# A two-layer decoder trunk in one kernel: the order of the last matmuls of each stage, and the variance of one half of the tokens by ScalarE

## The chip, the cores and the metric

The kernel runs on one core of a Trainium2 chip. The metric is the device time of one launch in microseconds (us), the median of several runs. TensorE (PE in the profile) does the matmuls, VectorE (DVE) and ScalarE (ACT) work elementwise, GpSimd (POOL) does small elementwise work and some loads, SyncE (SP) issues the weight loads. Each engine takes its own instructions in order; they wait for each other on semaphores.

## The reference, cut to what matters

The input is 256 tokens by 1024 channels in float32. Two layers run, each a sandwich of three steps; after each step there is a residual sum and a LayerNorm:

```python
for i in range(2):
    x = post_norm(x, 0.5 * swiglu(x, gate[i, 0], up[i, 0], down[i, 0]), g[i, 0], b[i, 0])
    mix = pool_mixer(...) if i == 0 else swa_sink_attention(...)
    x = post_norm(x, mix, g[i, 1], b[i, 1])
    x = post_norm(x, 0.5 * swiglu(x, gate[i, 1], up[i, 1], down[i, 1]), g[i, 2], b[i, 2])
# post_norm(x, sub) = layer_norm(alpha * x + sub), alpha = sqrt(2)
# swiglu(x) = (silu(x @ gate) * (x @ up)) @ down, 1024 -> 2816 -> 1024
```

So there are four SwiGLU stages (f = 0 to 3), one pooling mixer, one attention mixer, and six norms (n = 0 to 5): n = 0 after f = 0, n = 1 after the pooling, n = 2 after f = 1, n = 3 after f = 2, n = 4 after the attention, n = 5 at the very end.

## The kernel before, in words

**Tokens and banks.** The 256 tokens are two halves, t = 0 and t = 1, of 128 tokens, one to each partition. The sum of a stage stands in four PSUM banks, `ACC[t][h]`, h being the half of the 1024 output columns. `xn[:, t, :]` is the residual stream.

**Units.** The 2816 hidden channels are 22 units of 128. For each unit PE multiplies gate and up weights (`gate_up`), ACT and DVE make silu times up, then a high and a low part of it (`h_hi_of`, `h_lo_of`), and PE multiplies by the down weights (`ffn_down`, which calls `down`: three matmuls for each t and h, high by high, high by low, low by high). Weights are split likewise: ACT writes the high part of one half unit (`g_split`, L551) and DVE the low part (L860); for down weights L559 and L864. Unit 21 and units 0 and 1 are direct ones: ACT takes its silu from PSUM (L568), DVE multiplies (L875), ACT makes the high part (L578), DVE the low part (L880).

**The order is written by hand** for each engine, and so is each place of a `g_split`. In stages f = 1 and 2, unit 1 of the next stage's weights has its first half split last in unit 21: ACT's turn comes behind `h_hi_of`, DVE's behind `h_lo_of`. ACT splits the second half too, and POOL makes that half's low part (L384). ACT's `g_split` of that unit waits, before its first half, for

```python
after(act, g_used, G0[f] + (-1, 0, 0, 2)[u] if u < 4 else G - 1 + 4 * it)
```

where f and u are the next stage and 1; `g_used` reaches `G0[f]` with the last matmul of `gate_up` of unit 21 of the stage that ends. For the attention's weights the number is `G_QKV + 0`, with the same meaning.

**The end of a stage on PE** (last_u = 18), in order: the down matmuls of unit 19, t = 0, h = 1; of unit 18 for t = 1; of units 20 and 21 for t = 0, first h = 0 and then h = 1; of units 19 to 21 for t = 1, first h = 0 and then h = 1. The first down matmul of unit 21 waits for `h_lo_of(21)`. Then come the transposes of the normed t = 0 (L1328) and the next stage's first product over t = 0, `gate_up_tokens` (L1261), then the transposes of t = 1. After f = 0, PE runs the pooling: `means` (L1043) and `maps` (L1057) for t = 0 and 1. ACT copies the results of `means` into SBUF (L674). In the attention the last products are `wo(k)`, which also call `down`.

**A norm on DVE**, for t = 0 and then for t = 1: residual sum of h = 0 (L942), `bn_stats` of it (L948), the same for h = 1, `bn_aggr` (L952), variance plus epsilon (L953), which releases POOL's power of -1/2 (L450), the centring of both halves (L960, in place), the scaling of both halves (L973), which releases PE's transposes. `link` makes DVE wait for the instruction just issued. For t = 1 of all norms but the first and last, `x_lo` of t = 0 (L989) lies between variance and centring. ACT copies the transposed halves for the next stage (L630).

Of the kernel before, what the change touches and what calls it, by code (L numbers as in the profile page):

```python
# [21 lines left out]
P = 128  # L22
D = 1024
# [3 lines left out]
TT = S // P  # L27
UNITS = F // P
# [41 lines left out]
def trunk_kernel(nc, x, positions, ln_g, ln_b, w_gate, w_up, w_down, pool_w, pool_b, pool_scale,  # L70
# [8 lines left out]
    with ExitStack() as ctx:  # L79
# [28 lines left out]
        cst = sb("cst", [P, 4, P])  # L108
        stats = sb("stats", [P, 2, 6])
        mv = sb("mv", [P, 2, 2])  # L110
        rstd = sb("rstd", [P, 2, 2])
# [11 lines left out]
        xf = qT[:, :, :].rearrange("p k s -> p (k s)").rearrange("p (t k s) -> p t k s", t=TT, k=KT)  # L123
        uT = [v.rearrange("p (k s) -> p k s", k=KT) for v in (q_sb[:, :, :].rearrange("p t c -> p (t c)"), kT[:, :, :].rearrange("p g s -> p (g s)"))]
        pool_s = q_sb[:, :, :].rearrange("p t c -> p (t c)")
        pool_bs = kT[:, :, :].rearrange("p g s -> p (g s)")
# [27 lines left out]
        h_lo_done = sem("h_lo_done")  # L154
        acc_done = sem("acc_done")
        stat_done = sem("stat_done")
        cen_done = sem("cen_done")
# [379 lines left out]
        def _(act):  # L537
# [70 lines left out]
            def first_units(f):  # L608
# [9 lines left out]
                d_split(D0[f] + 2)  # L618

            def channel_major(e, between=None):  # L620

                for t in range(TT):
# [28 lines left out]
            for f in range(FFNS):  # L651
# [16 lines left out]
                if f == 0:  # L668

                    act.wait_ge(d_scaled, POOL_UNITS)  # L670
                    for t in range(TT):
# [7 lines left out]
                if f == 2:  # L679
                    channel_major(QKV_EVENT)  # L680
                    attention_act(act, g_split, d_split)
                    enter(3)

        def rotary_tables(dve, link):
# [158 lines left out]
        def _(dve):  # L843
# [38 lines left out]
            def unit(f, u, it=0):  # L882
# [53 lines left out]
            def residual_sum(n, t, h):  # L936
# [3 lines left out]
                if n == 4:  # L940
                    dve.wait_ge(res_done, t + 1)
                link(dve.scalar_tensor_tensor(xn[:, t, HALVES[h]], ACC[t][h], coef, xn[:, t, HALVES[h]], ALU.mult, ALU.add))  # L942

            def variance(n, t):

                for h in range(2):
                    residual_sum(n, t, h)
                    last = dve.bn_stats(stats[:, h, :], xn[:, t, HALVES[h]])  # L948
                    if h == 0:
                        note(last)  # L950
                link(last)
                link(dve.bn_aggr(mv[:, t, :], stats[:, :, :].rearrange("p a b -> p (a b)")))  # L952
                dve.tensor_scalar(rstd[:, t, 0:1], mv[:, t, 1:2], EPS / ALPHA ** 2, None, ALU.add).then_inc(stat_done, 1)  # L953

            def centre(n, t):

                if t == 0:
                    dve.wait_ge(scale_in, 16 * (n + 1))
                for h in range(2):
                    dve.scalar_tensor_tensor(xn[:, t, HALVES[h]], xn[:, t, HALVES[h]], mv[:, t, 0:1], ln_scale(n)[:, HALVES[h]],  # L960
                                             ALU.subtract, ALU.mult).then_inc(cen_done, 1)

            def scale(n, t):
# [7 lines left out]
                for h in range(2):  # L971
                    dve.wait_ge(cen_done, 4 * n + 2 * t + h + 1)
                    dve.scalar_tensor_tensor(xn[:, t, HALVES[h]], xn[:, t, HALVES[h]], rstd[:, t, 1:2], ln_offset(n)[:, HALVES[h]],  # L973
                                             ALU.mult, ALU.add).then_inc(xn_done if n < 5 else y_done, 1)
# [59 lines left out]

        def pool_pe(pe):

            def means(t, src, columns, first, last):

                for k in range(KT):
                    if k % 4 == 0 and t == src:  # L1040
# [3 lines left out]
                                    start=first and k % 4 == 0, stop=last and k % 4 == 3)  # L1044
                    if t == 0 and k == 0:
# [4 lines left out]
            def maps(t):  # L1050
                if t == 0:
                    pe.wait_ge(d_scaled, POOL_UNITS)
                for g in range(len(WINDOWS)):
                    if g % 2 == 0:
                        pe.wait_ge(u_sb, 2 * t + g // 2 + 1)
                    for j in range(2):
                        ins = pe.matmul(ACC[t][g // 2][:, (g % 2) * GC:(g % 2 + 1) * GC], uT[t][:, 2 * g + j, :],  # L1057
                                        pool_raw(j)[:, g * GC:(g + 1) * GC], start=j == 0, stop=j == 1)
                    if g % 2 == 1:
                        ins.then_inc(acc_done, 1)  # L1060
# [9 lines left out]
        def attention_pe(pe, three, down, transposes):  # L1070

# [94 lines left out]

            transposes(e, 0)
            qkv(0, 0, 0, part=0, d_counted=True)
            qkv(0, 1, 0, part=0)
# [46 lines left out]
            for h in range(2):  # L1216
                for k in range(5, 8):
                    wo(k, (1,), hs=(h,))
# [3 lines left out]
        def _(pe):  # L1222
# [28 lines left out]
            def gate_up_tokens(f, t):  # L1251
# [6 lines left out]
                for k in range(KT):  # L1258
                    if k % 4 == 0:
                        pe.wait_ge(x_hi_done, 4 * e + 2 * t + k // 4 + 1)  # L1260
                    pe.matmul(out_, xT_hi[:, k, tok], w_hi[:, :, :, k, :], start=k == 0, stop=False)  # L1261
                    pe.matmul(out_, xT_hi[:, k, tok], w_lo[:, :, :, k, :], start=False, stop=False)  # L1262
# [51 lines left out]
            def ffn_down(f, u, ts=(0, 1), it=0, hs=(0, 1)):  # L1314
# [6 lines left out]
                down(E, hT_hi[:, E % D_SLOTS, :], hT_lo[:, E % D_SLOTS, :], ts, u == 0, final, it, hs)  # L1321

            def transposes(e, t, used=0):

# [9 lines left out]
            for f in range(FFNS):  # L1334
                e = FFN_EVENT[f]

                transposes(e, 0, used=(0, 2, 1, 1)[f])
                if f == 0:
# [28 lines left out]
                ffn_down(f, last_u + 1, (0,), hs=(1,))  # L1367
                ffn_down(f, last_u, (1,))
                for h in range(2):
                    for u in (last_u + 2, last_u + 3):  # L1370
                        ffn_down(f, u, (0,), hs=(h,))
                for h in range(2):
                    for u in range(last_u + 1, UNITS):
                        ffn_down(f, u, (1,), hs=(h,))
                if f == 0:
                    pool_pe(pe)
                if f == 2:
                    attention_pe(pe, three, down, transposes)

# [38 lines left out]
```

## Time and profile before

| what | value |
|---|---|
| median of 3 runs | 860.23 us (860.13 to 860.37) |
| the profiled execution | 860.7 us |
| its span in the trace | 858.9 us |
| granted TensorE clock, mean | 0.997 |
| PE busy | 841.1 us, 98% of the span |
| PE weight loads busy (beside the matmuls) | 711.5 us, 83% |
| DVE busy | 562.8 us, 66% |
| ACT busy | 419.3 us, 49% |
| POOL busy | 45.8 us, 5% |
| chain that ended last | PE 91%, DVE 4%, ACT 1%, DMA 1% |

The span runs from the first to the last instruction on record; the profiled execution's own time is 1.8 us longer and lies 0.5 us above the median. Busy shares are means over the whole span. The ends of matmuls are modelled: two that overlap by the record stand about 0.23 us apart from start to start for 512 columns, and that is what one costs.

### The profile page before, as it was taken

The page shows a single profiled execution, that of the slowest core. Times are in us where ns is not written, and L with a number is a line of the kernel's source. Part 1 is how long each engine was busy: PE and PEld are TensorE (multiplying, and loading weights), DVE is VectorE, ACT ScalarE, POOL GpSimd, SP SyncE. Part 2 cuts the span into 40 slices and gives each one's busy share as a digit, 9 for nine tenths or more (in the row PEclk, how much of TensorE's full clock was granted, in tenths as well). Part 3 has the DMA queues.
Part 4 walks back from the last instruction along what each step waited for, and adds up shares of the span by engine and source line. Part 5 has one row for each costly group of instructions (what it writes and reads, how often), then busy time and mean ns, then how long its engine had stood idle before and what let it go on. Part 6 is the DMA issues. An engine that isn't in the chain of part 4 may idle for free.

```text
span 858.9 us, 12145 instructions
## 1 busy us (share of the span) xinstructions
PE 841.1 (98%) x4484; PEld 711.5 (83%) x4484; DVE 562.8 (66%) x777; ACT 419.3 (49%) x651; POOL 45.8 (5%) x59
## 2 busy tenths in 40 slices
PE   7999999999999999999999999999999999999995
PEld 6888888888888888887888888887766888888885
DVE  2785655669846565668665565669898855655656
ACT  2554454552535455454445454554665544454540
POOL 0060000013000000002000000011001000000000
PEclk9999999999999999999999999999999999999998
DMA  9997555392755655556656556553454565465501
GB/s 277 348 325 243 177 195 178 116 294 101 250 192 180 203 188 195 172 179 228 205 158 229 168 177 206 185 196 123 167 167 154 172 224 196 154 229 168 182 1 49
DMA packets 116142, 162.17 MB, mean 189 GB/s; under 512 B 3936, under 2 KB 97632, under 8 KB 116112
## 3 DMA queue, kind: packets, MB, share of 16 engines
q1 hardware_dynamic: 112656, 152.06, 53.1%
q0 software_dynamic: 2496, 9.44, 3.3%
q8 instruction: 19, 0.31, 0.1%
q10 hardware_dynamic: 960, 0.27, 0.1%
q14 instruction: 11, 0.09, 0.0%
HBM read 160.70 MB, written 1.05 MB: 188 GB/s over the span
## 4 chain that ended last, share of the span: by engine, by line
PE 91%; DVE 4%; SPq 1%; DMA 1%; ACT 1%; issue 1%; POOL 0%; DVEq 0%; ACTq 0%
PE ps L1295 29%; PE ps L1293 17%; PE ps L1226 10%; PE ps L1227 10%; PE ps L1228 10%; PE ps L1292 4%; PE ps L1261 1%; DMA raw_g<-in_ffn_w_up 1%; PE ps L1262 1%; PE ps L1266 1%; PE ps L1092 1%; PE ps L1095 1%; PE ps L1101 1%; SPq L322 1%; PE ps L1328 1%; PE ps L1057 1%
## 5 line engine op out<-in xcount | busy, mean ns | idle before, releaser
L1295 PE MATMUL ps<-xT,g_hi 128*128 128x512 f32 x1064 | 379.3, 396 | 0.0
L1293 PE MATMUL ps<-xT,g_lo 128*128 128x256 f32 x1216 | 314.2, 279 | 0.0
L1293 PEld LDWEIGHTS ps<-xT,g_lo 128*128 128x128 f32 x1216 | 229.2, 188 | 12.5
L860 DVE TENSOR_TENSOR g_lo<-raw_g,g_hi 128x1024 fp32r<-128x1024 f32 x179 | 220.4, 1235 | 24.9 <-ACT g_hi L551 24.9
L1295 PEld LDWEIGHTS ps<-xT,g_hi 128*128 128x128 f32 x1064 | 199.7, 188 | 41.2
L870 DVE TENSOR_TENSOR gu<-ps,gu 128x512 f32<-128x512 f32 x76 | 52.5, 691 | 221.9 <-ACT gu L574 221.9
L551 ACT ACTIVATE g_hi<-raw_g 128x1024 fp32r<-128x1024 f32 x184 | 192.1, 1052 | 5.2 <-DMA raw_g<-in_ffn_w_up 3.6
L574 ACT ACTIVATE gu<-ps 128x512 f32<-128x512 f32 x76 | 45.6, 600 | 273.5 <-PE ps L1295 273.5
L1226 PE MATMUL ps<-d_hi,hT_hi 128*128 128x512 f32 x352 | 137.5, 391 | 0.0
L1227 PE MATMUL ps<-d_lo,hT_hi 128*128 128x512 f32 x352 | 137.0, 389 | 0.0
L1228 PE MATMUL ps<-d_hi,hT_lo 128*128 128x512 f32 x352 | 137.0, 389 | 0.0
L864 DVE TENSOR_TENSOR d_lo<-raw_d,d_hi 128x1024 fp32r<-128x1024 f32 x96 | 117.3, 1224 | 5.9 <-ACT d_hi L559 5.8
L559 ACT ACTIVATE d_hi<-raw_d 128x1024 fp32r<-128x1024 f32 x96 | 99.8, 1046 | 4.7 <-DMA raw_d<-in_ffn_w_down 4.7
L1228 PEld LDWEIGHTS ps<-d_hi,hT_lo 128*128 128x128 f32 x352 | 66.1, 188 | 14.2
L1227 PEld LDWEIGHTS ps<-d_lo,hT_hi 128*128 128x128 f32 x352 | 66.1, 188 | 14.0
L1226 PEld LDWEIGHTS ps<-d_hi,hT_hi 128*128 128x128 f32 x352 | 66.1, 188 | 10.6
L1292 PE MATMUL ps<-xT,g_hi 128*128 128x512 f32 x152 | 60.4, 397 | 1.0 <-DVE g_lo L860 1.0
L578 ACT ACTIVATE hT_hi<-hf_sink 128x256 fp32r<-128x256 f32 x82 | 34.3, 418 | 34.5 <-DVE hf_sink L875 34.2
L880 DVE TENSOR_TENSOR hT_lo<-hf_sink,hT_hi 128x256 fp32r<-128x256 f32 x82 | 34.4, 420 | 3.4 <-ACT hT_hi L578 3.4
L875 DVE TENSOR_TENSOR hf_sink<-gu 128x256 f32<-128x256 f32 x76 | 33.3, 438 | 1.0 <-ACT gu L568 1.0
L568 ACT ACTIVATE gu<-gu 128x256 f32<-128x256 f32 x76 | 30.9, 407 | 3.2 <-DVE gu L870 3.2
L1292 PEld LDWEIGHTS ps<-xT,g_hi 128*128 128x128 f32 x152 | 28.5, 188 | 4.3 <-DVE g_lo L860 1.5
(155 smaller groups left out, 662.0 us busy)
## 6 DMA issues: line engine op xcount, KB each, us to landing
raw_d<-in_ffn_w_down SPq DMA_DIRECT2D x87, 512.0 KB, 4.0
raw_g<-in_ffn_w_gate SPq DMA_DIRECT2D x43, 1024.0 KB, 5.5
raw_g<-in_ffn_w_up SPq DMA_DIRECT2D x43, 1024.0 KB, 7.9
raw_g<-in_attn_w_qkv SPq DMA_DIRECT2D x6, 1024.0 KB, 6.3
raw_d<-in_attn_w_o SPq DMA_DIRECT2D x8, 512.0 KB, 3.8
gb<-in_ln_g POOLq DMA_DIRECT2D x5, 512.0 KB, 3.9
gb<-in_ln_b POOLq DMA_DIRECT2D x4, 512.0 KB, 5.8
xn<-in_x SPq DMA_DIRECT2D x2, 512.0 KB, 6.1
```

The source lines that it names most:

```text
L551: act.activation(g_half(g_hi, g_slot(f, u), half), src(G, half), ACT.Copy).then_inc(g_hi_done, 1)
L559: act.activation(d_hi[:, E % D_SLOTS, :], raw_d[:, (E // 2) % 2, E % 2, :], ACT.Copy).then_inc(d_hi_done, 1)
L574: act.activation(gu[:, u % 2, :, :], both[:, :, S:2 * S], ACT.Copy).then_inc(low_done, 1)
L860: dve.tensor_tensor(g_half(g_lo, g_slot(f, u), half), src(G, half), g_half(g_hi, g_slot(f, u), half).bitcast(f32), ALU.subtract).then_inc( ...
L864: dve.tensor_tensor(d_lo[:, E % D_SLOTS, :], raw_d[:, (E // 2) % 2, E % 2, :], d_hi[:, E % D_SLOTS, :].bitcast(f32), ALU.subtract).then_in ...
L870: dve.tensor_tensor(gu[:, u % 2, :, :], both[:, :, 0:S], gu[:, u % 2, :, :], ALU.add).then_inc(gu_done, 1)
L1226: pe.matmul(out_, l_hi, r_hi, start=start, stop=False)
L1227: pe.matmul(out_, l_hi, r_lo, start=False, stop=False)
L1228: return pe.matmul(out_, l_lo, r_hi, start=False, stop=stop)
L1292: pe.matmul(bank, w_hi, xT[:, k, :, :], start=True, stop=False)
L1293: last = pe.matmul(bank[:, S:2 * S], w_lo, xT_hi[:, k, :], start=False, stop=False)
L1295: last = pe.matmul(bank, w_hi, xT[:, k, :, :], start=False, stop=k == KT - 1)
```

## The change

On PE, each stage's last three matmuls (last unit, t = 1, h = 1) are taken out and put behind the next stage's transposes of t = 0. Ahead of them the order is by units: units 20 and 21 for t = 0 with both h, then for t = 1 units 18 to 21 of h = 0 and 18 to 20 of h = 1. In the attention the last `wo` product (k = 7, t = 1, h = 1) is moved likewise, and in the pooling the last group of `maps(1)`; the last SwiGLU stage has its three matmuls right behind the others. In the pooling `last_down(0)` stands behind `means` of t = 0.

In a norm, t = 0 has no `bn_stats`. Its residual sums also give row sums (`accum_out`), DVE makes minus the mean over 32 and then the mean, and ACT squares (x - mean)/32 over 1024 columns with a row sum, which is the variance. DVE centres t = 0 into another buffer (`centred`, in `q_sb`) meanwhile. Between variance and scaling of t = 0, DVE does the residual sum and `bn_stats` of h = 0 of t = 1, in all norms but n = 1.

In stages 1 and 2, both ACT's and DVE's split of the first half of the next stage's unit 1 is moved from the end of unit 21 to the end of unit 20.

```diff
@@ the split, on ACT @@
-                if f < 3 and u == UNITS - 1:
-                    g_split(*next_first(f, 1))
+                if f in (1, 2) and u == UNITS - 2:
+                    g_split(*next_first(f, 1), halves=(0,))
+                if f < 3 and u == UNITS - 1:
+                    g_split(*next_first(f, 1), halves=(0, 1)[f > 0:])
@@ the split, on DVE @@
-                if u == UNITS - 1:
-                    if f == 0:
-                        g_split(1, 0, halves=(1,))
-                    elif f < 3:
-                        g_split(*next_first(f, 1), halves=(0,))
+                if f == 0 and u == UNITS - 1:
+                    g_split(1, 0, halves=(1,))
+                elif f in (1, 2) and u == UNITS - 2:
+                    g_split(*next_first(f, 1), halves=(0,))
@@ ACT, called ahead of channel_major(n), before the pooling's copies (n = 0) and at the end (n = 5) @@
+            def squares(n):
+                act.wait_ge(mean_done, n + 1)
+                act.activation(squares_out, xn[:, 0, :], ACT.Square, bias=mv[:, 0, 1:2], scale=1.0 / 32,
+                               accum_out=rstd[:, 0, 0:1]).then_inc(var_done, 1)
@@ DVE @@
-                link(dve.scalar_tensor_tensor(xn[:, t, HALVES[h]], ACC[t][h], coef, xn[:, t, HALVES[h]], ALU.mult, ALU.add))
+                total = {"accum_out": sums[:, h:h + 1]} if t == 0 else {}
+                link(dve.scalar_tensor_tensor(xn[:, t, HALVES[h]], ACC[t][h], coef, xn[:, t, HALVES[h]], ALU.mult, ALU.add, **total))
+            def mean(n):
+                for h in range(2):
+                    residual_sum(n, 0, h)
+                dve.tensor_scalar(mv[:, 0, 1:2], sums[:, 0:1], sums[:, 1:2], -1.0 / (32 * D), ALU.add, ALU.mult).then_inc(mean_done, 1)
+                link(dve.tensor_scalar(mv[:, 0, 0:1], sums[:, 0:1], sums[:, 1:2], 1.0 / D, ALU.add, ALU.mult))
+            def half_stats(n, h):
+                residual_sum(n, 1, h)
+                link(dve.bn_stats(stats[:, h, :], xn[:, 1, HALVES[h]]))
...
-                for t in range(TT):
-                    variance(n, t)
-                    if t == 1 and between:
-                        between()
-                    centre(n, t)
-                    scale(n, t)
+                mean(n)
+                centre(n, 0)
+                variance(n, 0)
+                if n != 1:
+                    half_stats(n, 0)
+                scale(n, 0)
+                for h in range(n != 1, 2):
+                    half_stats(n, h)
+                variance(n, 1)
+                if between:
+                    between()
+                centre(n, 1)
+                scale(n, 1)
@@ PE @@
             means(0, 0, 0, True, True)
+            last_down(0)
             means(1, 0, P, True, False)
-            maps(0)
+            pool_maps(pe, 0, range(4))
             means(1, 1, S, False, True)
-            maps(1)
+            pool_maps(pe, 1, range(3))
...
-                transposes(e, 0, used=(0, 2, 1, 1)[f])
+                transposes(e, 0, used=(0, 2, 0, 0)[f])
+                if f == 1:
+                    pool_maps(pe, 1, (3,))
+                elif f == 2:
+                    last_down(1)
+                elif f == 3:
+                    down(D_WO + 7, xT_hi[:, 7, :], xT_lo[:, 7, :], (1,), False, True, hs=(1,))
...
-                ffn_down(f, last_u, (1,))
-                for h in range(2):
-                    for u in (last_u + 2, last_u + 3):
+                for u in (last_u + 2, last_u + 3):
+                    for h in range(2):
                         ffn_down(f, u, (0,), hs=(h,))
                 for h in range(2):
-                    for u in range(last_u + 1, UNITS):
+                    for u in range(last_u, UNITS - h):
                         ffn_down(f, u, (1,), hs=(h,))
```

The counting of `d_used` moves with the matmuls (into `gate_up_tokens` for f = 2 and 3, and into `means`), and `last_down(2)` stands behind the attention's transposes of t = 0.

## Rows read from the trace of the kernel before

**Rows 1.** The page's first part: busy time, share of the span, instructions.
```profile
PE 841.1 (98%) x4484; PEld 711.5 (83%) x4484; DVE 562.8 (66%) x777; ACT 419.3 (49%) x651; POOL 45.8 (5%) x59
```

**Rows 2.** Timeline, PE, end of stage 1: start us, us, engine, line, what.
```profile
387.38 0.40 PE L1226 MATMUL ps<-d_hi,hT_hi 128*128 128x512 f32 x1
...
396.26 1.32 PE L1328 MATMUL ps<-cst,xn 128*128 128x128 f32 x8
397.69 0.47 PE L1261 MATMUL ps<-g_hi,xT 128*128 128x512 f32 x1
```

**Rows 3.** Timeline, ACT, end of stage 1; in brackets idle before it and releaser.
```profile
387.57 0.38 ACT L568 ACTIVATE gu<-ps 128x256 f32<-128x256 f32 x1 [1.90 <-PE ps L1228]
```

**Rows 4.** Timeline, DVE, end of stage 1.
```profile
387.99 0.42 DVE L875 TENSOR_TENSOR hf_sink<-gu,ps 128x256 f32<-128x256 f32 x1 [1.06 <-ACT gu L568]
388.90 0.42 DVE L880 TENSOR_TENSOR hT_lo<-hf_sink,hT_hi 128x256 fp32r<-128x256 f32 x1 [0.48 <-ACT hT_hi L578]
391.00 0.69 DVE L942 SCALAR_TENSOR_TENSOR xn<-ps,xn 128x512 f32<-128x512 f32 x1
391.73 0.70 DVE L948 BATCH_NORM_STATS2 stats<-xn 128x6 f32<-128x512 f32 x1
394.06 0.15 DVE L953 TENSOR_SCALAR rstd<-mv 128x1 f32<-128x1 f32 x1
394.13 1.41 DVE L960 SCALAR_TENSOR_TENSOR xn<-xn,mv,gb 128x512 f32<-128x512 f32 x2
395.45 1.41 DVE L973 SCALAR_TENSOR_TENSOR xn<-xn,rstd,gb 128x512 f32<-128x512 f32 x2
```

**Rows 5.** Timeline, ACT and DVE, unit 20 of stage 2: a split ahead of a silu.
```profile
567.81 1.05 ACT L551 ACTIVATE g_hi<-raw_g 128x1024 fp32r<-128x1024 f32 x1
568.76 0.41 ACT L568 ACTIVATE gu<-gu 128x256 f32<-128x256 f32 x1
...
568.90 1.22 DVE L860 TENSOR_TENSOR g_lo<-raw_g,g_hi 128x1024 fp32r<-128x1024 f32 x1 [0.26 <-ACT g_hi L551]
570.04 0.42 DVE L875 TENSOR_TENSOR hf_sink<-gu 128x256 f32<-128x256 f32 x1
```

**Rows 6.** Timeline, POOL, end of stage 1.
```profile
394.30 1.00 POOL L450 TENSOR_TENSOR rstd<-rstd,mhalf 128x1 f32<-128x1 f32 x1 [0.67 <-DVE rstd L953]
```

**Rows 7.** Timeline, ACT, attention: an ACTIVATE that also gives a row sum.
```profile
629.78 0.40 ACT L480 ACTIVATE hf_sink<-hf_sink,sm 128x129 f32<-128x129 f32 x1
630.07 0.19 ACT L480 ACTIVATION_READ_ACCUMULATOR hf_sink<-hf_sink,sm 128x1 f32 x1
```

**Rows 8.** Timeline, pooling and entry of stage 1: PE, DVE, ACT.
```profile
188.72 0.40 PE L1226 MATMUL ps<-d_hi,hT_hi 128*128 128x512 f32 x1
206.57 3.68 PE L1057 MATMUL ps<-raw_d,kT 128*128 128x256 f32 x16
206.77 0.60 ACT L674 ACTIVATE kT<-ps 128x512 f32<-128x512 f32 x1 [0.30 <-PE ps L1043]
208.25 1.41 DVE L973 SCALAR_TENSOR_TENSOR xn<-xn,rstd,kx 128x512 f32<-128x512 f32 x2
211.47 0.47 PE L1261 MATMUL ps<-g_hi,xT 128*128 128x512 f32 x1 [0.34 <-ACT xT L630]
```

**Rows 9.** Timeline, end of the attention: PE, ACT, DVE.
```profile
656.57 0.50 PE L1226 MATMUL ps<-d_hi,xT 128*128 128x512 f32 x1
658.04 1.28 ACT L533 ACT_TABLE_LOAD   x1
662.98 1.41 DVE L973 SCALAR_TENSOR_TENSOR xn<-xn,rstd,aux 128x512 f32<-128x512 f32 x2
665.22 0.47 PE L1261 MATMUL ps<-g_hi,xT 128*128 128x512 f32 x1
```

**Rows 10.** Timeline, the last stage's end, DVE.
```profile
844.82 0.69 DVE L942 SCALAR_TENSOR_TENSOR xn<-ps,xn 128x512 f32<-128x512 f32 x1 [1.68 <-PE ps L1228]
854.99 1.41 DVE L973 SCALAR_TENSOR_TENSOR xn<-xn,rstd,gb 128x512 f32<-128x512 f32 x2
```

More of the change, by code:

```diff
@@ L155, in trunk_kernel @@
         acc_done = sem("acc_done")
+        mean_done = sem("mean_done")
+        var_done = sem("var_done")
         stat_done = sem("stat_done")
@@ L618, in first_units @@
                 d_split(D0[f] + 2)
+            def squares(n):
+                act.wait_ge(mean_done, n + 1)
+                act.activation(squares_out, xn[:, 0, :], ACT.Square, bias=mv[:, 0, 1:2], scale=1.0 / 32,
+                               accum_out=rstd[:, 0, 0:1]).then_inc(var_done, 1)
             def channel_major(e, between=None):
+                if e > 0:
+                    squares(e)
                 for t in range(TT):
@@ L668, in _ @@
                 if f == 0:
+                    squares(0)
                     act.wait_ge(d_scaled, POOL_UNITS)
@@ L682, in _ @@
                     enter(3)
+                if f == 3:
+                    squares(5)
         def rotary_tables(dve, link):
@@ L955, in centre @@
+            def variance(n, t):
+                if t == 0:
+                    dve.wait_ge(var_done, n + 1)
+                    var = rstd[:, 0, 0:1]
+                else:
+                    link(dve.bn_aggr(mv[:, 1, :], stats[:, :, :].rearrange("p a b -> p (a b)")))
+                    var = mv[:, 1, 1:2]
+                dve.tensor_scalar(rstd[:, t, 0:1], var, EPS / ALPHA ** 2, None, ALU.add).then_inc(stat_done, 1)
             def centre(n, t):
                 if t == 0:
+                    if n == 0:
+                        dve.wait_ge(d_scaled, POOL_UNITS)
@@ L1033, in _, with pool_maps, pool_pe @@
                     layer_norm(5)
-        def pool_pe(pe):
+        def pool_maps(pe, t, groups):
+            if t == 0:
+                pe.wait_ge(d_scaled, POOL_UNITS)
+            for g in groups:
+                if g % 2 == 0:
+                    pe.wait_ge(u_sb, 2 * t + g // 2 + 1)
+                for j in range(2):
+                    ins = pe.matmul(ACC[t][g // 2][:, (g % 2) * GC:(g % 2 + 1) * GC], uT[t][:, 2 * g + j, :],
+                                    pool_raw(j)[:, g * GC:(g + 1) * GC], start=j == 0, stop=j == 1)
+                if g % 2 == 1:
+                    ins.then_inc(acc_done, 1)
+        def pool_pe(pe, last_down):
             def means(t, src, columns, first, last):
@@ L1044, in means @@
                                     start=first and k % 4 == 0, stop=last and k % 4 == 3)
-                    if t == 0 and k == 0:
+                    if t == 1 and src == 0 and k == 0:
                         ins.then_inc(d_used, 1)
@@ L1048, in means @@
                         ins.then_inc(u_done, 1)
[L1050 to L1060, printed above, removed]
             pe.wait_ge(band_in, 16)
@@ L1064, in pool_pe, with attention_pe @@
             means(0, 0, 0, True, True)
+            last_down(0)
             means(1, 0, P, True, False)
-            maps(0)
+            pool_maps(pe, 0, range(4))
             means(1, 1, S, False, True)
-            maps(1)
-        def attention_pe(pe, three, down, transposes):
+            pool_maps(pe, 1, range(3))
+        def attention_pe(pe, three, down, transposes, last_down):
             ident = cst[:, 0, :]
@@ L1216, in attention_pe @@
             for h in range(2):
-                for k in range(5, 8):
+                for k in range(5, 8 - h):
                     wo(k, (1,), hs=(h,))
@@ L1260, in gate_up_tokens @@
                         pe.wait_ge(x_hi_done, 4 * e + 2 * t + k // 4 + 1)
-                    pe.matmul(out_, xT_hi[:, k, tok], w_hi[:, :, :, k, :], start=k == 0, stop=False)
+                    ins = pe.matmul(out_, xT_hi[:, k, tok], w_hi[:, :, :, k, :], start=k == 0, stop=False)
+                    if f > 1 and t == 0 and k == 0:
+                        ins.then_inc(d_used, 1)
                     pe.matmul(out_, xT_hi[:, k, tok], w_lo[:, :, :, k, :], start=False, stop=False)
@@ L1321, in ffn_down, with last_down @@
                 down(E, hT_hi[:, E % D_SLOTS, :], hT_lo[:, E % D_SLOTS, :], ts, u == 0, final, it, hs)
+            def last_down(f):
+                ffn_down(f, UNITS - 1, (1,), hs=(1,))
             def transposes(e, t, used=0):
@@ L1367, in _ @@
                 ffn_down(f, last_u + 1, (0,), hs=(1,))
-                ffn_down(f, last_u, (1,))
-                for h in range(2):
-                    for u in (last_u + 2, last_u + 3):
+                for u in (last_u + 2, last_u + 3):
+                    for h in range(2):
                         ffn_down(f, u, (0,), hs=(h,))
                 for h in range(2):
-                    for u in range(last_u + 1, UNITS):
+                    for u in range(last_u, UNITS - h):
                         ffn_down(f, u, (1,), hs=(h,))
                 if f == 0:
-                    pool_pe(pe)
+                    pool_pe(pe, last_down)
                 if f == 2:
-                    attention_pe(pe, three, down, transposes)
+                    attention_pe(pe, three, down, transposes, last_down)
+                if f == 3:
+                    last_down(f)
 _INS = ["x", "positions", "ln_g", "ln_b", "ffn_w_gate", "ffn_w_up", "ffn_w_down", "pool_w", "pool_b", "pool_scale",
```

17 lines of the change are left out of this document (8 added, 9 removed).

## The prediction

> **What bounds the kernel now.** First the page's busy shares: PE has matmuls in 98% of the span, DVE 66%, ACT 49% [rows 1]. So work taken from DVE or ACT brings nothing by itself. What can be had is PE's idle time at the joins of stages, and what follows its last matmul. I then read the timelines around each join, engine by engine.
>
> At the end of stage 1, PE runs its last 39 down matmuls from 387.38 to 396.26, 0.2275 us each, goes into the transposes at once and starts the next stage at 397.69 [rows 2]: 1.43 us for eight transposes that need 0.9 (an estimate: a 256-column float32 matmul costs 3.68/16 = 0.23 [rows 8], so 128 columns about 0.11). That join has about 0.5 us to give. The others look alike (next stage at 211.47 and 665.22 [rows 8, 9]), so the five joins hold about 2.2 us in all. The tail holds more: the last norm's DVE work runs from 844.82 to 856.4 [rows 10], while PE, at 0.2275 for each of its last 24 matmuls, ends near 850.1.
>
> Beside this stands how tight the last unit is. ACT waits 1.90 us idle for the last gate and up matmul and starts silu(21) at 387.57 [rows 3]; DVE multiplies at 387.99 and gives the low part from 388.90 to 389.32 [rows 4].
>
> **The change, part by part.** I write S1 for the start of token half 0's second residual sum, M for the first mean instruction.
>
> *The new norm's length.* A linked 512-column pass takes 0.73 us from start to start (391.00 to 391.73 [rows 4]). A sum that also gives a row sum has no row here. Below, its surcharge is 0; above, 0.19, ACT's separate read of its accumulator [rows 7]. I take 0.1, between the two as nothing is nearer. The Trainium skill, VectorE: DVE Perf Modes, section on two Vector instructions with no wait between them, says that an op that also writes out its accumulator is two instructions; no run here shows it for DVE, and by it the sum would stand nearer the 0.19. So M = S1 + 0.83. ACT begins at M + 0.19 (a 0.15 us instruction and 0.04 of hand-over, as from DVE's end at 388.41 to ACT's next). The square over 1024 columns has no row: at least a plain one, 1.05 [rows 5]; at most 0.40 for 129 columns [rows 7] plus 895 columns at 0.00086 each, 1.17. With 0.08 us for the end of the read, 1.13 to 1.25; I take 1.24. The variance is there at M + 1.43, hidden behind DVE's centring, two passes of 1.32 together [rows 4], which end DVE's turn at M + 1.57. POOL's power then takes from 394.06 to 395.30 plus hand-over [rows 4, 6]: 1.29. So the scaling can start at M + 2.86 = S1 + 3.69; meanwhile DVE does sum and statistics of t = 1, h = 0, which take 1.46 once that bank is done.
>
> *The order of PE's last matmuls.* The t = 0 banks are done after matmuls 12 and 15 instead of 15 and 21; t = 1, h = 0 after 27. From a bank's last matmul to DVE's sum go 0.22 us.
>
> *The moved split, stages 1 and 2.* ACT's split of the next unit 1 waits for the end of gate_up(21), the very thing silu(21) waits for, and now stands ahead of it. So at 387.57 ACT starts a split, not the silu. Rows 5 show that order: the silu follows 0.95 later, DVE's split starts 1.09 after ACT's, and DVE's product 1.14 after that. Queued behind are silu(21), the product, ACT's high part, DVE's low part, and PE's first down matmul of unit 21. The product starts at 387.57 + 1.09 + 1.14 = 389.80 instead of 387.99, 1.81 late; the low part ends at 391.13. PE comes to unit 21 after 9 matmuls, at 389.43, and gets it at 391.17: it stalls 1.74 us. Before, it came there after 12 and had 0.7 us to spare. Stages 0 and 3 keep their splits and come out even (389.43 against 389.36, by the same rows).
>
> *Join after stage 1.* Banks of t = 0 are seen by DVE at 392.07 and 392.76; S1 = 392.90, M = 393.73, variance handed over at 395.30. Bank (1, 0) is seen at 391.17 + 18 x 0.2275 + 0.22 = 395.49; sum and statistics until 396.95; scaling from there. PE's transposes follow 0.81 later (395.45 to 396.26 [rows 2, 4]): 397.76, while its own matmuls ended at 397.31. The second four wait for DVE, 0.66 later, and take 0.45; then the moved three matmuls, 0.68: the next stage starts at 399.55 against 397.69. ACT's copies lie beside these three matmuls, so they cost nothing. At the transposes of t = 1 a wait of 0.17 goes, since PE is later: **+1.7 us**. Join after stage 2 is the same pattern: **+1.7**.
>
> *Pooling.* From 188.72 [rows 8]: banks seen at 191.67 and 192.35, S1 = 192.50, bank (1, 0) at 195.08, scaling at 196.54, means at 197.35 against about 197.7; then 0.68 for the moved matmuls: PE is 0.3 late for the rest. Norm 1 is the trouble: squares(1) stands in ACT's queue behind the copies of t = 1's means, the last of which starts at 206.77 + 0.3 [rows 8]. Squares start 0.5 later, 207.57; variance 208.81; scaling 210.14 instead of 208.25; transposes 210.95, second four 211.61 to 212.06, one map of four (3.68/4 = 0.9 [rows 8]) to 212.95, against 211.47: **+1.5**. The copies cannot hide it, for PE has only six eighths of its maps left.
>
> *Join after the attention.* t = 0 is not done sooner here: bank (0, 1) after 12 of 30 matmuls, 656.57 + 2.73 + 0.1 for its slower first + 0.22 = S1 = 659.6. M = 660.45, variance over at 662.0, sum and statistics to 663.55 against scaling at 662.98 [rows 9]; transposes 664.35, second four 665.0 to 665.45, moved matmuls to 666.15 against 665.22. Less 0.15 at t = 1: **+0.8**.
>
> *Tail.* Here bank (0, 1) is seen when (0, 0) was, 844.82 [rows 10]; S1 = 844.97, M = 845.80; bank (1, 0) at 844.82 + 2.73 = 847.55; scaling of t = 0 at 849.01; DVE free at 850.33; the last bank is seen at 850.28. Then sum 0.73, statistics 0.73, aggregate 0.24, variance 0.07, centring 1.32: scaling at 853.42 instead of 854.99 [rows 10]: **-1.6**. One sum with its statistics, 1.4 us, has gone ahead into the gap.
>
> *The rest costs nothing:* the centring's other output has the same size (cover: none needed, same pass); two 1-column instructions are in M; POOL's half split ends by about 394.1, before 395.30; SP's next gate and up loads wait for that split, 0.4 us later than at 393.6, and without cover would cost those 0.4. No DMA issue is moved.
>
> **The sum:** 1.5 + 1.7 + 1.7 + 0.8 - 1.6 = +4.1 us. Against the profiled execution that is 860.7 + 4.1 = 864.8; the median of the runs lies 0.5 lower: 864.3.
>
> **The rivals.** *The split does not delay unit 21* (its wait is met sooner than I read the count). For it: a half split would fit in ACT's 1.90 idle us [rows 3]. Against: silu(21) ends that idle time at just the count that the split asks for. Joins 1 and 2 then give 0.0 to +0.1 less 0.17, and the sum is 1.5 - 0.2 + 0.8 - 1.6 = +0.5: 860.7. *Faster: the moved three matmuls fill every join.* Place: between PE's transposes and next stage. Price: the 2.2 us of idle there and 1.6 of the tail, 856.4. It decides in its favour if DVE's scaling of t = 0 starts by PE's shorter end less 0.81, 394.8 in stage 1 even with no stall; I get 395.2 there without the stall, and at the attention's join 663.55 where it would take 662.0. *Square is not in the table that ACT holds.* A table load takes 1.28 us [rows 9]; one ahead of each of six squares gives +7.7 more, 872. Against: copies run between silu and exp with no load of their own. ScalarE: Activation LUTs, of the Trainium skill, section on table sets, asks for about 2.7 us for each switch; the trace's 1.28 decides.
>
> **How the numbers follow.** My forecast 0.70, with 863 to 865.8 as its own range (surcharge 0 to 0.19 and the square's bounds move each of four joins by some 0.1 to 0.2; the 0.4 of the load comes on top). The split rival 0.15, the filled joins 0.08, the table 0.03, and 0.04 for smaller stalls of both signs. To leave out no more than 2 in 10 the range takes in the split rival: 860.5 to 866. Some 0.2%, 1.7 us, is what a measurement of this kernel can tell from no change: slower by more 0.75, within it 0.16, faster 0.09.
>
> **What would show it.** In the trace after: ACT L551 directly ahead of the silu of unit 21 in stages 1 and 2, and a PE wait of about 1.7 us for the low part in each, none in stages 0 and 3; PE waiting about 1.3 us for the transposes after the pooling, 0.4 to 0.8 at other joins; about 1.6 us less from PE's last matmul to the end. No stall in unit 21, or squares(1) ahead of 207, would make me wrong.

## The result and the profile after

The changed kernel takes 867.19 us (865.27 to 867.34, 4 runs), the kernel before 860.18 us beside it: 1.0077 times as long, 95% interval 1.0064 to 1.009. The forecast was 864.3 with a range to 866.0. So the direction was right, the size too small and the time outside the range.

The page of the changed kernel, busy shares, granted clock and the PE groups of the down product (columns as in [rows 1]; the idle time ahead of the group and its releaser stand last):

```profile
PE 843.6 (97%) x4484; PEld 713.4 (82%) x4484; DVE 558.5 (65%) x783; ACT 426.4 (49%) x663; POOL 43.1 (5%) x59
...
L1269 PE MATMUL ps<-d_hi,hT_hi 128*128 128x512 f32 x352 | 138.1, 392 | 3.3 <-DVE hT_lo L898 3.3
```

The work of each engine is what it was [rows 1]; ACT has 7 us more for six squares, DVE 4 us less. But PE now waits: this group had 0.0 us of idle time ahead of it on the page before, and now has 3.3, released by DVE's low part of a hidden unit. PE's list of waits, longest first in total (who waited for whom: us, times, longest), names the other one; ahead of these lines it has only the load of the masks at the kernel's start:

```profile
PE ps L1269 <- DVE hT_lo L898: 3.3, 2, 1.6
PE ps L1376 <- DVE xn L1006: 3.1, 4, 1.7
PE ps L1096 <- DVE xn L1006: 0.7, 1, 0.7
```

L1376 are the transposes at a join, L1096 the pooling's means; both wait for the scaling of the first token half. Here is the end of stage 1, one view for each engine, as in [rows 2 to 4, 6]. ACT first:

```profile
388.82 1.06 ACT L556 ACTIVATE g_hi<-raw_g 128x1024 fp32r<-128x1024 f32 x1 [1.96 <-PE ps L1271]
389.78 0.37 ACT L573 ACTIVATE gu<-ps 128x256 f32<-128x256 f32 x1
391.50 0.42 ACT L583 ACTIVATE hT_hi<-hf_sink 128x256 fp32r<-128x256 f32 x1 [1.35 <-DVE hf_sink L893]
```

ACT idles as long as before, 1.96 us, and then does a split (L556) and not the silu (L573). DVE:

```profile
389.91 1.23 DVE L878 TENSOR_TENSOR g_lo<-raw_g,g_hi 128x1024 fp32r<-128x1024 f32 x1 [1.79 <-ACT g_hi L556]
391.05 0.41 DVE L893 TENSOR_TENSOR hf_sink<-gu,ps 128x256 f32<-128x256 f32 x1
391.95 0.43 DVE L898 TENSOR_TENSOR hT_lo<-hf_sink,hT_hi 128x256 fp32r<-128x256 f32 x1 [0.48 <-ACT hT_hi L583]
393.43 0.69 DVE L960 SCALAR_TENSOR_TENSOR xn<-ps,xn 128x512 f32<-128x512 f32 x1 [1.06 <-PE ps L1271]
394.05 0.08 DVE L960 DVE_READ_ACCUMULATOR xn<-ps,xn 128x1 f32 x1
394.19 0.69 DVE L960 SCALAR_TENSOR_TENSOR xn<-ps,xn 128x512 f32<-128x512 f32 x1
...
396.63 0.15 DVE L982 TENSOR_SCALAR rstd<-rstd 128x1 f32<-128x1 f32 x1
396.86 0.69 DVE L960 SCALAR_TENSOR_TENSOR xn<-ps,xn 128x512 f32<-128x512 f32 x1
397.59 0.69 DVE L972 BATCH_NORM_STATS2 stats<-xn 128x6 f32<-128x512 f32 x1
398.32 1.41 DVE L1006 SCALAR_TENSOR_TENSOR xn<-q_sb,rstd,gb 128x512 f32<-128x512 f32 x2
```

And PE:

```profile
390.40 0.39 PE L1271 MATMUL ps<-d_hi,hT_lo 128*128 128x512 f32 x1
392.43 0.50 PE L1269 MATMUL ps<-d_hi,hT_hi 128*128 128x512 f32 x1 [1.64 <-DVE hT_lo L898]
...
398.48 0.39 PE L1271 MATMUL ps<-d_hi,hT_lo 128*128 128x512 f32 x1
399.13 1.32 PE L1376 MATMUL ps<-cst,xn 128*128 128x128 f32 x8 [0.26 <-DVE xn L1006]
400.20 0.47 PE L1269 MATMUL ps<-d_hi,hT_hi 128*128 128x512 f32 x1
...
400.97 0.40 PE L1304 MATMUL ps<-g_hi,xT 128*128 128x512 f32 x1
```

From 390.40 to 392.43 are 2.03 us for a matmul that costs 0.23: a stall of 1.80. The three moved matmuls at 400.20 do fill the time of ACT's copies, and the scaling of the first half follows the statistics of the second half's first columns without a gap. What was moved works as meant; what it costs lies ahead of it.

What I had no term for shows at the join after the attention. PE:

```profile
667.85 0.39 PE L1271 MATMUL ps<-d_hi,xT 128*128 128x512 f32 x1
669.91 1.32 PE L1376 MATMUL ps<-cst,xn 128*128 128x128 f32 x8 [1.67 <-DVE xn L1006]
670.98 0.62 PE L1269 MATMUL ps<-d_hi,xT 128*128 128x512 f32 x1
671.40 0.63 PE L1270 MATMUL ps<-d_lo,xT 128*128 128x512 f32 x1
671.83 0.63 PE L1271 MATMUL ps<-d_hi,xT 128*128 128x512 f32 x1
672.26 0.63 PE L1304 MATMUL ps<-g_hi,xT 128*128 128x512 f32 x1
```

and the busy time by stretches (us, then busy PE, PEld, DVE, ACT, POOL with their instructions, granted clock, DMA share, GB/s):

```profile
655.00:671.10 16.10, 13.84 (x70) 9.86 (x69) 12.84 (x24) 9.69 (x20) 2.96 (x2) 1.00 0.39 130
671.20:674.60 3.40, 3.40 (x10) 2.63 (x9) 2.00 (x5) 2.49 (x3) 0.17 (x1) 0.50 0.96 302
674.60:700.00 25.40, 25.15 (x127) 21.03 (x127) 19.10 (x24) 11.47 (x16) 1.50 (x3) 1.00 0.51 169
```

The granted clock is 0.50, that is 1.2 GHz instead of 2.4, for 3.4 us, in which PE never waits: matmuls that take 0.23 us from start to start take 0.43. Half of 3.4, 1.7 us, is lost. It falls some 1.2 us after PE came out of 2.06 us without a matmul. The kernel before has no such stretch: its clock stays at 1.00 from 10.3 us until 853.4 us, which is behind PE's last matmul.

The distances between stage entries (first matmul over the normed first half; first of the last 39 down matmuls for the start of the first line) set against the forecast's terms:

| part | before, us | after, us | measured | forecast |
|---|---|---|---|---|
| pooling: 188.72 to 211.47; 188.23 to 212.47 | 22.75 | 24.24 | +1.5 | +1.5 |
| stage 1, to 397.69; to 400.97 | 186.22 | 188.50 | +2.3 | +1.7 |
| stage 2, to 583.78; to 589.15 | 186.09 | 188.18 | +2.1 | +1.7 |
| attention, to 665.22; to 672.26 | 81.44 | 83.11 | +1.7 | +0.8 |
| stage 3, to PE's last matmul, 849.83; 857.91 | 184.61 | 185.65 | +1.0 | 0 |
| tail, to the end of the span | 9.07 | 7.44 | -1.6 | -1.6 |

With 0.5 us less ahead of the first line, which comes from the kernel's start and differs from run to run, this is the span's +6.5.

### The profile page after: what moved, and what is told of

It reads as the page before. It is cut to its first block, busy times and chain, and to the rows that moved or that the text cites. A ratio compares the mean times of both kernels' runs of the same rounds, so it can differ in the third digit from the quotient of the medians.

```text
span 865.4 us, 12180 instructions
## 1 busy us (share of the span) xinstructions
PE 843.6 (97%) x4484; PEld 713.4 (82%) x4484; DVE 558.5 (65%) x783; ACT 426.4 (49%) x663; POOL 43.1 (5%) x59
## 4 chain that ended last, share of the span: by engine, by line
PE 91%; DVE 5%; ACT 1%; DMA 1%; issue 1%; POOL 0%; DVEq 0%; SPq 0%; ACTq 0%
PE ps L1340 29%; PE ps L1338 16%; PE ps L1269 10%; PE ps L1270 10%; PE ps L1271 10%; PE ps L1337 4%; PE ps L1304 1%; PE ps L1307 1%; PE ps L1311 1%; PE ps L1289 1%; PE ps L1134 1%; PE ps L1137 1%; PE ps L1143 1%; PE ps L1376 1%; DVE xn L1006 1%; DVE xn L960 1%
## 5 line engine op out<-in xcount | busy, mean ns | idle before, releaser
L556 ACT ACTIVATE g_hi<-raw_g 128x1024 fp32r<-128x1024 f32 x184 | 192.0, 1050 | 8.4 <-PE ps L1271 3.9
L573 ACT ACTIVATE gu<-gu 128x256 f32<-128x256 f32 x76 | 30.9, 407 | 3.2 <-DVE gu L888 3.2
```

Source lines behind the costliest of these rows:

```text
L556: act.activation(g_half(g_hi, g_slot(f, u), half), src(G, half), ACT.Copy).then_inc(g_hi_done, 1)
```

## The experiments

Theory A, taken from this: two stalls by the moved split, a late norm at the mixers' joins, and a fall of TensorE's clock after PE's long idle time at the attention's join. Rivals are named with each run. Runs with and without the fall of the clock are told apart by their time and their mean granted clock together, within one kernel, and I give both groups where both occur. The mean alone does not do it, since it also counts the half clock behind PE's last matmul: the profile of e2 has a mean of 0.996 and no fall before its end.

**Undo the moved split.** In stages 1 and 2, in the changed kernel:

```diff
-                if f in (1, 2) and u == UNITS - 2:
-                    g_split(*next_first(f, 1), halves=(0,))
-                if f < 3 and u == UNITS - 1:
-                    g_split(*next_first(f, 1), halves=(0, 1)[f > 0:])
+                if f < 3 and u == UNITS - 1:
+                    g_split(*next_first(f, 1))
@@ DVE @@
-                elif f in (1, 2) and u == UNITS - 2:
+                elif f in (1, 2) and u == UNITS - 1:
```

> The changed kernel with one part undone: in stages 1 and 2 the first half of the next unit 1 is split by ACT and DVE in unit 21 again. Theory A (the split ahead of silu(21) stalls PE 1.81 us in each of the two stages): both stalls vanish; DVE's first residual sum then waits for the split as it did before, so each of the two joins keeps some 0.5 us; 3.2 us less than the changed kernel, about 864.0 if TensorE's clock falls in the attention's join as in the changed kernel's trace, 862.1 if it does not. Rival B (the stall only takes the place of a wait for DVE's norm at the join): under 1 us less, 866.3 or more.

Measured: 863.62 us (863.27 to 863.89, 5 runs), ratio to the kernel before 1.004 (1.0027 to 1.0054), mean clock 0.998 in all five. Both stalls are gone from the trace. But against the changed kernel's one run with full clock, 865.27, that is 1.65 us and not 3.6: about half of each stall comes back as waiting at the join, where PE now stands idle until DVE has scaled (1.67 us from its last matmul to the transposes in both stages, against 0.65 in the changed kernel). At full clock I had expected 862.1, so Theory A holds for the stalls and not for the gain, and rival B, under 1 us, falls too. DVE's view shows why:

```profile
391.83 0.69 DVE L958 SCALAR_TENSOR_TENSOR xn<-ps,xn 128x512 f32<-128x512 f32 x1
...
393.66 2.02 DVE L990 SCALAR_TENSOR_TENSOR q_sb<-xn,mv,gb 128x512 f32<-128x512 f32 x2
```

and POOL's, in the same kernel:

```profile
392.07 2.40 POOL L389 TENSOR_TENSOR g_lo<-raw_g,g_hi 128x1024 fp32r<-128x1024 f32 x1 [172.91 <-DVE g_lo L876]
```

The first sum waits for the split, as I had reckoned, but the two centring passes take 2.02 us instead of 1.41 [rows 4].

**The moved split alone**, in the kernel before (the same lines, the other way):

> The kernel before with only the split of stages 1 and 2 moved to unit 20. Theory A: PE gets to unit 21 three matmuls later than in the changed kernel (390.11 in stage 1) and its low part comes at 391.17 to 391.22, so it stalls 1.1 us in each stage and nothing gives it back: +2.1 us, 862.3. Rival B: the stall is absorbed by PE's idle 0.5 us at each join: +1.2 us, 861.4. No stall at all: 860.2.

Measured: 862.67 us (862.09 to 863.11, 8 runs), ratio 1.0026 (1.0016 to 1.0037). The stall of stage 1 in PE's timeline:

```profile
388.86 0.39 PE L1229 MATMUL ps<-d_hi,hT_lo 128*128 128x512 f32 x1
390.21 0.50 PE L1227 MATMUL ps<-d_hi,hT_hi 128*128 128x512 f32 x1 [0.96 <-DVE hT_lo L882]
```

1.35 from start to start, 1.1 of it stall, and the same in stage 2 (576.41 to 577.77). So Theory A holds here: +2.4 us against the 2.1 expected, nothing is given back.

**The attention's join as before**, in the changed kernel:

```diff
-                for k in range(5, 8 - h):
+                for k in range(5, 8):
@@ entry of stage 3 @@
-                elif f == 3:
-                    down(D_WO + 7, xT_hi[:, 7, :], xT_lo[:, 7, :], (1,), False, True, hs=(1,))
@@ norm 4: bn_stats for both token halves, as in the kernel before @@
```

> The changed kernel with the attention's join as before (norm 4 by bn_stats, the last wo matmuls in their old place). Theory A (PE's idle 2.06 us there is what lets the granted clock fall to half for 3.4 us): the clock stays full, and both the idle and the half-speed matmuls go: 1.3 + 1.9 = 3.2 us less, 864.0. Rival C (the clock falls by the sum of all stalls before, not by this gap): it falls here too, 865.9.

Measured: 864.24 us (863.91 to 864.51, 5 runs), clock 0.998 or 0.999 in all. That is 3.0 less than the changed kernel's median; Theory A's 864.0 stands and rival C's 865.9 falls. The stalls of stages 1 and 2 are still there, 2.03 us from start to start, and in these five runs they do not bring the clock down.

**The attention's join alone**, in the kernel before:

> The kernel before with only norm 4 and the last wo matmuls changed. Theory A: PE idles about 1.5 to 1.9 us there; +1.2 us by itself, and the granted clock falls in at least some runs, which adds 1.9: 861.4 or 863.3. Rival C: without the other stalls the clock stays full in every run, 861.4.

Measured: 861.4 us median, in two groups: eight runs at 861.08 to 861.82 (clock 0.997 or 0.998) and three at 863.16 to 863.58 (0.995). One join with 2.06 us without a matmul and a full clock costs 1.1 us (median of the eight 861.32); the same join brings 1.9 more in 3 of 11 runs. So it takes no other stall for the clock to fall, and rival C falls for good. The fall does not come in every run with the same idle time; e1 has that idle time and none in five.

**Fill the idle time.** The changed kernel with two matmuls into an unused bank (their result is not read; they stand as four records in the view):

```diff
+                if f == 3:
+                    for _ in range(2):
+                        pe.matmul(ps[:, WORK + 2, :], ident, cst[:, :, :].rearrange("p m q -> p (m q)"), start=True, stop=True)
                 transposes(e, 0, used=(0, 2, 0, 0)[f])
```

> The changed kernel with two more matmuls (identity by the four constant masks, 512 float32 columns each, into a bank that nobody reads) ahead of the transposes in the attention's join, where PE idles 2.06 us. Theory A (PE's idle time there is what lets the granted clock fall in most runs): the two take about 1.7 us of the idle time, the clock stays full in every run, and all runs stand at 865.3, as the one run of the changed kernel with full clock. Rival F (the clock falls by chance or by the load of the chip, whatever PE does there): most runs at 867.2 or above.

Measured: 865.4 us (864.57 to 865.97, 5 runs), clock 0.998 or 0.999 in all five, where three of four runs of the changed kernel had 0.996. PE at the join:

```profile
667.17 0.40 PE L1271 MATMUL ps<-d_hi,xT 128*128 128x512 f32 x1
667.40 1.88 PE L1387 MATMUL ps<-cst 128*128 128x512 f32 x4
669.22 0.99 PE L1376 MATMUL ps<-cst,xn 128*128 128x128 f32 x5
```

More work on PE makes the kernel 1.8 us faster than the changed kernel's median. Five runs alone would not settle it, since e1 kept the idle time and had no fall in five either. All kernels together do: with the 2.06 us at this join (the changed kernel, e1, e4, e7, e8, e10) the time and the clock show the fall in 17 of 42 runs, without it (e2, e3, e5, e9, e11) in none of 40. PE's idle time at this join is what lets the clock fall. Why the stalls of 2.03 us amid down matmuls do not is left open: this idle time lies ahead of transposes, and no run changes that alone. Three runs of kernels without the idle time stand out for no reason that I can show, as they have no profile: two of the 61 of the kernel before beside the experiments (861.82 and 862.78, clock 0.995 and 0.996) and one of e6 (861.55, 0.997).

**The tail alone**: the kernel before with the last stage's new order and norm 5 in the new form.

> The kernel before with the change at the very end alone: the last SwiGLU stage's order of down matmuls and norm 5. My theory (the tail's term of the sum, -1.57 us, is right and independent of the joins): 1.6 us less than the kernel before, 858.6; in the trace the last scaling starts 3.6 us after PE's last matmul begins instead of 5.2. Rival: the tail only looked shorter because the stage before it was late; no gain, 860.2.

> As e5_tail_only, but norm 5 by bn_stats for both halves as before: only the order of PE's last 39 down matmuls of the last stage is changed. Theory: the first half's norm starts 0.68 us earlier and the chain on DVE has the old length, so 0.7 us less than before, 859.5; the other 0.9 us of e5 come from the squares on ACT and the second half's sum in the gap. Rival (the order is all of it): 858.6.

Measured: 858.66 us (858.06 to 858.92, 11 runs), ratio 0.998 (0.9971 to 0.9989), with both; 859.52 us, ratio 0.9994 (0.9985 to 1.0003), 11 runs, with the order alone. By the times alone the order cannot be told from no change; the trace shows what it does. The last scaling in DVE's timeline, e5 and then e6:

```profile
852.39 1.41 DVE L1008 SCALAR_TENSOR_TENSOR xn<-xn,rstd,gb 128x512 f32<-128x512 f32 x2
```

```profile
853.79 1.41 DVE L1008 SCALAR_TENSOR_TENSOR xn<-xn,rstd,gb 128x512 f32<-128x512 f32 x2
```

PE's last matmuls start at 848.82 and 849.35, so the scaling follows 3.57 and 4.44 us later, against 5.16 before [rows 10, PE's last at 849.83]: 0.7 us by the order, 0.9 by the new norm, 1.6 together, as expected, and both rivals fall. e5 beats both kernels.

**Norm 1 as before**, on top of e1 (bn_stats for both token halves):

> e1_split_back with norm 1 (after the pooling) by bn_stats as before, all else the same. Theory (squares(1) comes late because it stands in ACT's queue behind the copies of the second half's means, and norm 1 has nothing in its gap): PE's wait for the transposes after the pooling goes from 1.3 us to 0.3 or less, 0.9 us less than e1: 862.7. Rival (PE waits there because the banks themselves are late by the moved matmuls): 863.6 as e1.

Measured: three runs at full clock, 862.37 to 863.10, and three with the fall, 864.17 to 864.68 (0.996). Against e1 at full clock 0.6 us less. In the traces, the distance from the 36th of stage 0's last matmuls to the entry of stage 1 is 15.35 us here (196.23 to 211.58) and 16.16 in e1 (195.97 to 212.13): 0.8 of the 0.9 expected, and the rival falls. The run takes the whole new norm out at this place, so it prices that norm there; that the squares stand behind the copies is read from ACT's view of the changed kernel:

```profile
207.18 0.60 ACT L690 ACTIVATE kT<-ps 128x512 f32<-128x512 f32 x1 [0.30 <-PE ps L1096]
207.68 1.14 ACT L630 ACTIVATE gu<-xn,mv 128x1024 f32<-128x1024 f32 x1
```

**POOL's half split moved to DVE**, on top of e1:

```diff
                 scale(n, 0)
+                if n in (2, 3):
+                    g_split(*next_first(n - 1, 1), halves=(1,))
@@ POOL @@
-                    elif t == 0 and n in (2, 3):
-                        low_half(*next_first(n - 1, 1), 1)
```

> e1_split_back with the second half's split of the next unit 1 in stages 1 and 2 done by DVE after it scaled the first token half, instead of by POOL during the norm. Theory D (DVE's centring of two SBUF operands is slowed by POOL's split beside it: 2.02 us for two passes against 1.41): centring takes 1.41 again, PE's transposes come 0.6 us earlier in each of two joins, and DVE has 1.4 idle us there that take the 1.2 us split: 1.2 us less than e1, 862.4. Rival E (the long centring comes from ACT's square reading the same rows at the same time): centring stays at 2.0, and 863.6 or more.

Measured: three runs at full clock, 862.20 to 862.57, and three with the fall, 864.00 to 864.54. Centring in stage 1:

```profile
394.22 1.42 DVE L988 SCALAR_TENSOR_TENSOR q_sb<-xn,mv,gb 128x512 f32<-128x512 f32 x2
```

1.42 us with ACT's square still beside it (394.10 to 395.25), 1.42 in stage 2 too, and 862.4 at full clock, as expected. So it was POOL, and rival E falls.

**Let the split wait for less.** The changed kernel, but the moved split's wait asks for 21 units' gate and up matmuls and not 22, since unit 21 reads another buffer:

```diff
-                        after(act, g_used, G_QKV + (-1, 0, 0, 1, 3, 4)[u])
+                        after(act, g_used, G_QKV + (-1, -1, 0, 1, 3, 4)[u])
-                        after(act, g_used, G0[f] + (-1, 0, 0, 2)[u] if u < 4 else G - 1 + 4 * it)
+                        after(act, g_used, G0[f] + (-1, -(f == 2), 0, 2)[u] if u < 4 else G - 1 + 4 * it)
```

> The changed kernel with ACT's split of the next unit 1 (stages 1 and 2) waiting for 21 units of gate and up instead of 22; the buffer that it writes is not read by unit 21. Theory A: the split then runs in ACT's idle 1.9 us ahead of silu(21), which is on time; both stalls of 1.81 us go, DVE's first sum starts 0.7 us earlier than in e1, and POOL's half split is over before DVE's centring: 4.0 us less than the changed kernel at the same clock: 861.3, or 863.2 in runs in which the clock falls. Rival (the split ahead of the silu delays it anyway): 1 us less or under.

Measured: five runs at full clock, 861.34 to 862.35, and five with the fall, 862.91 to 863.37. ACT at the end of stage 1:

```profile
386.21 1.04 ACT L556 ACTIVATE g_hi<-raw_g 128x1024 fp32r<-128x1024 f32 x1
388.20 0.38 ACT L573 ACTIVATE gu<-ps 128x256 f32<-128x256 f32 x1 [0.95 <-PE ps L1271]
```

The split lies in ACT's idle time, the silu starts as soon as PE is done, and both stalls are gone: 3.4 us less than the changed kernel's one run at full clock, of 4.0 expected. The rival falls. One number in each of two waits was worth 3.4 of the 5.1 us that the change costs at full clock.

> As e10, with the two joins around the mixers (norms 0, 1 and 4, the last matmuls of stage 0, the pooling and the attention) as before, so that the change stands only in the joins after stages 1 and 2 and at the end. Theory A: the joins then break even within 0.1 us each against the kernel before and the tail gives its 1.6 us: 858.5, full clock in every run. Rival (moving the three matmuls behind the transposes does shorten a join): under 858.0.

Measured: 859.17 us (858.59 to 860.18, 11 runs), ratio 0.999 (0.9981 to 0.9999), every run at 0.997 to 0.999. With its waits right, the change at the two SwiGLU joins brings nothing. By its trace the distances between entries there are 186.39 and 186.40 us, against 186.22 and 186.09 before, 0.2 and 0.3 more and not the 0.1 that I had allowed; the median is 0.5 above that of the tail alone, though the two intervals overlap. The rival, under 858.0, falls.

## Why the prediction was right and wrong

**Right: the signs and the places.** The split ahead of silu(21) stalls PE by 1.80 us in each of stages 1 and 2 (forecast 1.74), and none in stages 0 and 3; e2 and e10 show it from both sides. The tail is 1.6 us shorter (e5). The rival in which the split does not delay unit 21 is refuted, as is the one in which moved matmuls fill every join (e11), and there is no table load at the squares. The surcharge for a row sum that I took as 0.1 is a second instruction of 0.08 us, DVE_READ_ACCUMULATOR, and sums with it stand 0.72 to 0.77 apart where plain ones had stood 0.73: at most 0.04, near 0 and far from the 0.19 of ACT's. The Trainium skill, VectorE: DVE Perf Modes, section Two Vector instructions with no wait between them, says that such an op is two instructions; that is what the trace shows.

**Right by luck: the pooling.** The term was +1.5 and the join gave +1.5, but parts of it were wrong and cancel. POOL's split makes the centring of norm 0 take 1.98 us instead of 1.41, the whole pooling is late by it, and squares(1) starts 19.45 us behind the first of the last 39 down matmuls and not 18.85: 0.6 too little. Against that, POOL's power takes 0.56 us and not the 1.00 that I took from the trace before, so the scaling follows the variance (208.94) after 0.89 and not 1.29; and from the transposes to the entry are 1.74 us, not 2.00.

```profile
191.45 2.41 POOL L389 TENSOR_TENSOR g_lo<-raw_g,g_hi 128x1024 fp32r<-128x1024 f32 x1 [6.93 <-DVE g_lo L878]
193.10 1.98 DVE L992 SCALAR_TENSOR_TENSOR q_sb<-xn,mv,gb 128x512 f32<-128x512 f32 x2
209.18 0.56 POOL L455 TENSOR_TENSOR rstd<-rstd,mhalf 128x1 f32<-128x1 f32 x1 [3.07 <-DVE rstd L982]
```

The signs that I named for the joins were off too: PE waits 0.9 us for the transposes after the pooling (1.3 forecast), 0.3 in stages 1 and 2 and 1.7 after the attention (0.4 to 0.8 forecast).

**Wrong: no term for the clock.** The step that failed is the attention join's term of +0.8 with nothing behind it for stage 3: by its own times PE idles there for 1.5 us (own matmuls over at 662.8, transposes at 664.35), and the sum counts that idle time as itself and the stage behind it as unchanged. Three of four runs lose 1.9 to 2.1 us more than the fourth; in the trace it is half of 3.4 us at half clock, spread over the end of that join and the first matmuls of stage 3, which come out +1.7 and +1.0 instead of +0.8 and 0. With it the changed kernel stands at 867.2, without at 865.3 (the one run; e9 has 865.4), which lies inside the range. So of the 2.9 us between forecast and measurement some 1.9 are the clock and the other 1.0 the terms below. The range should have had a case "long idle time, lower clock". The longest time without a matmul at full clock in the trace before is 1.43 us (26.84 to 28.27), after which nothing fell; it could not price a longer one, and I did not bound it.

**Wrong by 0.4 to 0.6 us each: stages 1 and 2.** The term was +1.7 and measured +2.3 and +2.1. In stage 1 the parts are: after the stall PE's first matmuls are slower (0.33 and 0.24 from start to start against 0.23), which with a stall of 1.80 for 1.74 has the bank seen some 0.2 us late and the scaling with it; the credit of 0.17 at the transposes of the second half did not come, since they and ACT's copies take 1.29 us there (406.43 to 407.72) as before (1.28); and the way from the stage's entry to its last 39 matmuls is 0.2 longer, 0.1 of it at the first matmul (0.42 from start to start, 0.30 before).

**Wrong by 0.3: the attention's join.** Its centring starts at 666.04 while POOL's split runs until 666.47, and takes 1.56 us up to the next instruction instead of 1.32:

```profile
664.07 2.40 POOL L389 TENSOR_TENSOR g_lo<-raw_g,g_hi 128x1024 fp32r<-128x1024 f32 x1 [17.96 <-DVE g_lo L878]
666.04 1.64 DVE L992 SCALAR_TENSOR_TENSOR q_sb<-xn,mv,gb 128x512 f32<-128x512 f32 x2
```

I had checked that POOL is free in time for the power, and not what its split does to DVE beside it.

**A claim that holds only in part.** I wrote that the split costs 1.8 us by stalling PE. In the full change about half of it cannot be won by moving the split back (e1), because the new norm's centring then falls into POOL's split. It can be won by the wait's number (e10).

## What to carry to other kernels

When a step is moved ahead of another in an engine's queue, look first at what its own wait asks for: if it asks for the same event that its new neighbour waits for, the neighbour is late by the whole step, however idle the engine was before. Price a new idle time on PE in two cases, with and without a lower clock behind it, and look for changes that shorten the work behind PE's last matmul: here that part alone was worth its full 1.6 us. And when two engines' steps come to lie side by side, ask what they share: the terms of the pooling and of the attention's join both missed that POOL's split slows DVE's centring.

## What the runs showed of the hardware

PE's granted clock can fall to half after about 2 us without a matmul: in the changed kernel, e7, e8 and e10 (profiles of each) it fell for 3.4 us, 0.8 to 1.6 us after PE had resumed; in the profiles of e1 and e4, with the same 2.06 us from the last matmul's start to the first transpose's, it did not. Within one kernel the two groups of runs differ by 1.3 to 2.0 us. The stalls of 2.03 us from start to start in stages 1 and 2 never brought it down in a profile (the changed kernel, e3, e9), nor did the 1.67 us ahead of the transposes of stages 1 and 2 in e1 and e7. So the length without a matmul does not decide by itself, and what does is not shown here.

DVE and POOL get in each other's way. The two centring passes, which read two SBUF operands, take 1.41 us alone, 1.64 in the attention's join, where POOL's split overlaps them for the first 0.43 us, and 2.02 in e1, with 0.81 us of overlap. In norm 0 of the changed kernel it is 1.98 with 0.76 us of overlap. In all three DVE's passes grow by the overlap less 0.2 us. Sums out of PSUM beside the same split keep their 0.69. It goes the other way too: POOL's power over one column takes 1.00 us where DVE centres beside it (394.30 before, 202.09 after) and 0.56 where DVE sums out of PSUM or is idle (396.85 and 209.18 after). The Trainium skill, SBUF — State Buffer, section Who interferes with whom, says that a DVE instruction with two SBUF inputs contends with a GpSimd instruction that reads SBUF, and one with at most one SBUF input, outside the two-port modes, does not. These rows agree.

The square over 1024 columns with its row sum took 1.16 us and 0.18 for the read, 1.24 together, and ran in the table that was loaded for silu.
